# Entering the second block of a two-block network without a pause: modulation, the second stream's features and the final norm moved beside other work

## The reference

```python
def first_block(x, ...):
    for l in range(2):
        x = x + 0.5 * swiglu(rmsnorm(x, norm_ffn1[l]), w_ffn1_in[l], w_ffn1_out[l])
        ...                                      # mixer of three attentions
        x = x + 0.5 * swiglu(rmsnorm(x, norm_ffn2[l]), w_ffn2_in[l], w_ffn2_out[l])
    return rmsnorm(x, norm_final)

def second_block(x, c, ctx, c_ctx, ...):
    for i in range(2):
        sh1x, sc1x, g1x, sh2x, sc2x, g2x = silu(c) @ ada_w[i] + ada_b[i]      # 1024 x 6144
        sh1c, ... = silu(c_ctx) @ ada_w[i] + ada_b[i]
        hx = rmsnorm_2(x, norm_g[i, 0]) * (1 + sc1x) + sh1x
        hc = rmsnorm_2(ctx, norm_g[i, 0]) * (1 + sc1c) + sh1c
        if i == 0:      # Fourier mixing: fft2 over rows and groups of 256 columns, then fnet_wo
            x, ctx = x + g1x * fourier_mix(hx), ctx + g1c * fourier_mix(hc)
        else:           # RWKV, x alone is updated
            x = x + g1x * rwkv(hx, hc)
        x = x + g2x * ec_moe(rmsnorm_2(x, norm_g[i, 1]) * (1 + sc2x) + sh2x)  # 16 experts
        if i == 0:
            ctx = ctx + g2c * ec_moe(...)
    return rmsnorm_2(x, final_g)
```

## Time and profile before

| | us |
|---|---|
| median of 3 runs (lowest, highest) | 3563.28 (3561.82, 3569.27) |
| profiled execution, its own time | 3555.66 |
| its span, first to last instruction | 3553.6 |
| TensorE busy in it | 2912.4 (82%) |
| VectorE busy / ScalarE busy | 1184.2 / 973.2 |

### The profile page before, as it was taken

One profiled execution on the slowest core, in us unless ns is written; L12 is line 12 of the kernel. 1 busy time (PEld: TensorE's weight loads), 2 busy tenths in 40 slices (PEclk: granted clock), 3 DMA queues, 4 the chain that ended last, 5 costly groups with the idle time before them and its releaser, 6 DMA issues.

```text
span 3553.6 us, 63013 instructions
## 1 busy us (share of the span) xinstructions
PE 2912.4 (82%) x27818; PEld 1931.8 (54%) x27818; DVE 1184.2 (33%) x1569; ACT 973.2 (27%) x1474; POOL 179.9 (5%) x227
## 2 busy tenths in 40 slices
PE   8998999999989996798888873977878785677765
PEld 6776777787767774543333222436767673433322
DVE  4455565454555543130000014124343334100001
ACT  4445444343454441221000001013333330100000
POOL 0002000000020000000000000012221210000000
PEclk9999999999999998899999996989899898777787
DMA  6442345656423457029999981210000001699997
GB/s 246 169 178 98 114 172 190 238 194 248 153 104 128 178 195 288 8 71 399 421 421 421 421 337 80 95 64 9 8 9 14 8 4 40 269 421 421 421 421 300
DMA packets 100699, 708.62 MB, mean 199 GB/s; under 512 B 11572, under 2 KB 12340, under 8 KB 16992
## 3 DMA queue, kind: packets, MB, share of 16 engines
q1 hardware_dynamic: 94320, 682.34, 48.7%
q10 hardware_dynamic: 5472, 19.91, 1.6%
q0 software_dynamic: 656, 2.52, 0.2%
HBM read 703.65 MB, written 1.07 MB: 198 GB/s over the span
## 4 chain that ended last, share of the span: by engine, by line
PE 57%; DMA 21%; DVE 9%; issue 7%; ACT 4%; POOL 2%; SPq 0%; ACTq 0%; DVEq 0%; POOLq 0%
DMA weight_ring<-in_stream 19%; PE banks L536 7%; PE banks L538 7%; PE banks L537 7%; PE banks L1743 7%; PE banks L347 4%; PE banks L844 2%; PE banks L1619 2%; PE banks L846 2%; PE banks L845 2%; PE banks L2181 1%; PE banks L1651 1%; PE banks L2230 1%; PE banks L973 1%; ACT scratch L2547 1%
## 5 line engine op out<-in xcount | busy, mean ns | idle before, releaser
L1743 PE MATMUL banks<-weight_ring,scratch 128*32 128x256 f32 (+1 forms) x4608 | 630.5, 527 | 194.2 <-DMA weight_ring<-in_stream 190.4
L1743 PEld LDWEIGHTS banks<-weight_ring,scratch 128*32 128x32 f32 (+1 forms) x4608 | 200.8, 133 | 604.7 <-DMA weight_ring<-in_stream 301.6
L533 DVE TENSOR_TENSOR split_high<-weight_ring,split_high 128x1024 fp32r<-128x1024 f32 x198 | 243.4, 1230 | 272.3 <-ACT split_high L528 270.9
L528 ACT CAST split_high<-weight_ring 128x1024 fp32r<-128x1024 f32 x198 | 207.9, 1052 | 302.9 <-PE banks L538 265.8
L2547 ACT COPY scratch<-banks 128x1024 f32<-128x1024 f32 (+2 forms) x208 | 154.5, 766 | 306.1 <-PE banks L2234 126.7
L1167 DVE TENSOR_TENSOR split_high<-weight_ring,split_high 128x1024 fp32r<-128x1024 f32 x128 | 160.0, 1256 | 198.4 <-ACT split_high L1062 198.0
L1860 DVE TENSOR_TENSOR scratch<-scratch,banks 128x512 f32<-128x512 f32 (+1 forms) x32 | 17.7, 554 | 607.4 <-PE banks L1743 607.4
L536 PE MATMUL banks<-split_high,features_low 128*128 128x512 f32 x528 | 211.1, 400 | 3.3 <-DVE features_low L455 3.3
L538 PE MATMUL banks<-split_high,features_high 128*128 128x512 f32 x528 | 207.4, 393 | 0.0
L537 PE MATMUL banks<-split_high,features_high 128*128 128x512 f32 x528 | 207.2, 392 | 0.0
L844 PE MATMUL banks<-split_high,features_low 128*128 128x512 f32 x416 | 170.1, 409 | 19.5 <-DVE split_high L1167 16.2
(11 more groups left out here) (347 smaller groups left out, 4800.7 us busy)
## 6 DMA issues: line engine op xcount, KB each, us to landing
weight_ring<-in_stream SPq DMA_DIRECT2D x648, 1024.0 KB, 11.4
scratch<-in_pair_rows ACTq DMA_DIRECT2D x8, 448.0 KB, 3.8
scratch<-in_lora ACTq DMA_DIRECT2D x2, 1536.0 KB, 12.7
front<-in_gain_rows ACTq DMA_DIRECT2D x5, 512.0 KB, 4.2
bias<-bias_rows POOLq DMA_DIRECT2D x1, 2304.0 KB, 14.1
scratch<-in_routing ACTq DMA_DIRECT2D x2, 1040.5 KB, 5.1
scratch<-in_ada_b ACTq DMA_DIRECT2D x2, 768.0 KB, 3.9
resid<-in_x SPq DMA_DIRECT2D x2, 512.0 KB, 3.7
```

The lines of the kernel that those rows point to most:

```text
L528: act.copy(split[i % 4][0], source(i)).then_inc(*self.rounded.up())
L533: dve.tensor_tensor(lo, source(i), hi.bitcast(F32), ALU.subtract).then_inc(*self.rest.up())
L1743: last = pe.matmul(self.psum[q * M:(q + 1) * M, (GATE, UP, DOWN)[part], 0:W], left, w[:, j * D + q * W:j * D + (q + 1) * W], start=(k == 0 ...
```

## The change

- The modulation groups move: group 0 is now multiplied in stage 0, group 1 in stage 2, group 2 in stage 3, none in stage 5. Groups 3, 4 and 5 (24 chunks) all stand in front of RWKV: group 3 in `modulation_first`, groups 4 and 5 in `modulation_rest`, which is called between RWKV's norm and its features.
- A new class `Early` runs inside stage 5: it loads `ctx`, the bias, `norm_g`, the final gain and `dft`, finishes the modulation of layer 0, and makes the features `hT` of `ctx`. Its steps hang on the eleven groups of the up product by their number `n`.
- `fourier` has no `meet` in front any more. It transforms the eight pieces of `ctx` first, and does the last stage's `finish`, the final norm, the block's norm and the features of `x` beside them, row tile by row tile.
- The small tables `turns` of the mixer move to the tile `small`, and the saved modulation rows to `ada`.

```diff
+class Early:
+    def on_act(self, act, n):
+        if n == 0:
+            # six loads: ctx (2), ada_b, norm_g, norm_final, dft
...
+        elif n == 2:
+            act.wait_ge(p.consts_loaded.sem, self.consts)
+            for t in range(TT):
+                act.activation(self.xn[:, t, :], p.resid[:, (2 + t) * D:(3 + t) * D], ACT.Square, accum_out=self.sums[:, t:t + 1])\
+                    .then_inc(*self.up("ctx_squared"))
+        elif n == 3:
+            self.wait(act, "ctx_meant", 1)
+            act.activation(self.roots, self.sums, ACT.Sqrt).then_inc(*self.up("ctx_rooted"))
+        elif n in (6, 7):
+            t = n - 6
+            self.wait(act, "mod_ready", 1)
+            self.wait(act, "ctx_turned", t + 1)
+            for k in range(KT):
+                last = act.activation(self.hT[:, k, t * P:(t + 1) * P], p.psum[:, 6 + k // 4, (k % 4) * P:(k % 4 + 1) * P],
+                                      ACT.Identity, bias=p.modcol[:, 0, 1, k:k + 1], scale=p.scol[:, 0, 1, k:k + 1])
+            last.then_inc(*self.up("ctx_featured"))
+    def on_pe(self, pe, n):
+        if n in (3, 4):
+            if n == 3:
+                self.wait(pe, "mod_added", 1)
+            else:
+                self.wait(pe, "mod_copied", 2)
+            for g in ((0, 1), (2,))[n - 3]:
...
+                    last = pe.transpose(p.psum[:, 6 + g % 2, b * P:(b + 1) * P], self.mod[:, g, b * P:(b + 1) * P], p.ident[:, :])
+        elif n in (6, 7):
...
+                last = pe.transpose(p.psum[:, 6 + k // 4, (k % 4) * P:(k % 4 + 1) * P], self.xn[:, t, k * P:(k + 1) * P], p.ident[:, :])
+    def on_dve(self, dve, n):
+        if n == 2:
...
+            dve.tensor_tensor(self.mod_all, self.mod_all, self.bias, ALU.add).then_inc(*self.up("mod_added"))
+        elif n == 3:
+            self.wait(dve, "ctx_squared", 2)
+            dve.tensor_scalar(self.sums, self.sums, 1.0 / D, EPS, ALU.mult, ALU.add).then_inc(*self.up("ctx_meant"))
+        elif n in (4, 5):
+            for g in ((0, 1), (2,))[n - 4]:
+                self.wait(dve, "mod_turned", g + 1)
+                p.copy_mod(dve, g, 6 + g % 2).then_inc(*self.up("mod_copied"))
...
@@ ffn, TensorE / ScalarE (VectorE likewise, at the end of its group n)
             for n in range(1, groups):
+                if inner is not None:
+                    inner.on_pe(pe, n - 1)
                 if n >= 2:
                     pe.wait_ge(self.hid_done.sem, hid0 + n - 1)
...
                     self.save_bias(act, n - 2)
+                if inner is not None:
+                    inner.on_act(act, n)
@@ modulation
+    def modulation_groups(self, groups, chunk, bias, cT):
+            for i, g in enumerate(groups):
+                for k in range(KT):
+                    self.ada_chunk(pe, chunk + KT * i + k, k, cT, g)
+            for i, g in enumerate(groups):
+                pe.wait_ge(ve.sem, added0 + i + 1)
...
@@ fourier, TensorE
+            for i, (t, g) in enumerate(first):            # first: ctx's pieces, then x's
+                if i in (2, 5):
+                    turn(i // 3)
+                if i in (8, 12):
+                    wait(pe, self.parts_high, (i - 4) // 4)
+                if i >= 4:
+                    wait(pe, self.saved, i - 3)
@@ experts
-            if layer == 0:
-                for k in range(KT):
-                    self.ada_chunk(pe, a0 + k, k, self.silu_c, 0)
@@ rwkv_inputs
         self.norm_rows(range(n_t), xn)
+        self.modulation_rest()
         self.to_features(xn, hT, n_t, ...)
@@ run
-            self.ffn(3 * layer, ada=1 if layer else None)
+            self.ffn(3 * layer, ada=2 if layer else 0)
...
-            self.ffn(3 * layer + 2, ada=2 * layer)
+            self.ffn(3 * layer + 2, ada=None if layer else 1, inner=Early(self) if layer else None)
...
-        self.final_norm("norm_final", lambda t: self.resid[:, t * D:(t + 1) * D])
-        self.ada_group(3, before)
...
-        self.move_ada()
-        self.load_ctx()
-        self.modulation(0)
         self.experts(0, *self.fourier())
-        self.modulation(1)
+        self.modulation_first()
```

## The result

The changed kernel takes 3507.2 us (median of 4 runs, 3501.3 to 3513.89), the kernel before 3562.55 on the same chip (median of 4): a ratio of 0.9844, 95% interval 0.9827 to 0.9862. It is 55 us faster; forecast were 47, and 3516 in a range of 3503 to 3531. The profiled execution is 3501.3, its span 3499.3, against 3553.6. Left out of what follows are two of the four executions of experiment 4, 4225.53 and 3742.27 us, which ran at a mean granted clock of 0.675 and 0.79 where the other two had 0.91.

A forecast was written before the change was run, and what follows sets the result against it. TensorE was taken as busy for 82% of the span, so its standstills count, chiefly the break between the blocks. -71.6 + 0.8 + 9.8 - 5.7 + 19.8 = -46.9, from the median 3563.28 to 3516 us, range 3503 to 3531.

The forecast's parts named there:

- The break: Between stage 5's last matmul and the second transform: loads and waits leave the chain, 104.9 + 0.6 becomes 33.9, -71.6 us.
- the bound that the text had at 10.65: At the break: if TensorE finds its first piece only when the second tile is normed, the gain is 10.65 less, 61.
- The rival in which the seam waits for `x`: First transform: ScalarE's list holds up each piece, 10.65 more, up to 15: 3527 to 3531 us; chance 0.15.
- Stage 5: Group 2's chunks leave (-9.8); transposes (+3.1), a wait behind group 4 (+4.5) and slower clock (+3.0) come: +0.8 us.
- both terms: Behind group 4 of stage 5: a TensorE wait of 4.5 us, then 3.0 us for the lower clock.
- The rival of four waits: Stage 5: `Early` waits at each of its four places, three more of 7.5 each: 3538 us; chance 0.10.
- Stage 0: Group 0's eight chunks enter there in the same pattern, 8 x 1.23: +9.8 us.
- In front of RWKV: RWKV's entry: 16 more chunks must land before the features, so L290 starts at 2180.3 instead of 2160.55: +19.8 us.
- One sign: Between the last expert and RWKV's features the stream was to run at 421 GB/s without a pause.
- The experts' start: Layer 0's experts: group 3's eight chunks leave; first chunk used 14.2 later, 19.9 less to load: -5.7 us.
- lower bound of -9: At the experts' start: -9 us if the gather, which stands behind short waits, runs at a higher clock.

The follow-up runs named there:

- experiment 4: The kernel before, with only modulation group 3 moved from in front of layer 0's experts to in front of RWKV: 3567.88 and 3575.78 us.
- Experiment 3: The changed kernel with the first transform's pieces of `x` ahead of those of `ctx`: 3514.22 us, ratio 0.9873.
- experiment 1: The changed kernel with group 4 still multiplied ahead of RWKV's features and group 5 behind them: 3496.41 us, ratio 0.9805.
- experiment 6: The changed kernel with RWKV's four parameter loads issued earlier, ahead of the engines' meeting: 3507.92 us, ratio 0.9855.
- early loads: The changed kernel with RWKV's parameter loads issued ahead of the meeting; its three profiles took 794.6, 790.1 and 788.5 us from low-rank product to final projection.
- experiment 7: Four more profiles, two each of the changed kernel and that with earlier parameter loads: executions 3504.28, 3515.67, 3503.25 and 3501.41 us.

## Why the prediction was right

- **The break, -71.6: measured -72.4.** The list of waits came out as worked out: second tile normed at 10.0 (forecast 10.65), gates over at 33.4 (33.9). The features of `x`'s first tile, which hold up the second square, ended 7.6 behind the end of the stage (8.0). Experiment 3 shows that the order `ctx` first is worth 7 to 8 of it, the bound that the text had at 10.65. The rival in which the seam waits for `x` did not come.
- **Stage 5, +0.8: measured +0.4.** The wait was 4.5, as forecast, the clock behind it 0.52 for 5 us, and taking the wait away gave 7.2 against the 7.5 that both terms had. `Early`'s other three places did not wait: the list of TensorE's waits from 1180 to the end of the stage names L142 once, and L152 not at all. The Trainium skill ("ScalarE: Activation LUTs", What ACT_TABLE_LOAD costs) counts a drain of some 1.38 on top of a load of some 1.28, by which the wait would have been 5.9, an estimate; here the load of 1.28 starts 0.02 behind the cast, the silu 0.01 behind the load, and the wait is 4.5, so the measurement decides against the drain for this switch. Inside the 4.5 two sizes were off and cancelled: the load put the product 0.75 later and not 0.65, and the eight copies took 0.59 and not 0.8. (The rival of four waits had a slip in its sum: 3516.4 and three times 7.5 are 3539, not 3538.)
- **Stage 0, +9.8: measured +10.2.** That the two agree to 0.4 is in part luck: the end of stage 0 lies between 227.2 and 230.3 in seven profiles of kernels with the same code there.
- **In front of RWKV, +19.8: measured +20.7**, and +20.4 with group 3 alone moved (experiment 4). The bytes set it: experiment 1 takes eight of the 24 chunks out of the wait and wins 16, experiment 6 only fills idle transfer time and wins 6. One sign did not come: the stream was to run at 421 GB/s without a pause, and it ran at shares of 0.54 and 0.83 for the first 24 us (experiment 6 shows the two stretches). The sum did not suffer, since it was counted from a chunk that had the same pause ahead of it before (a share of 0.54 from 2111.00 to 2115.80).
- **The experts' start, -5.7: measured -12.5, with -1.0 in the experts themselves.** This is the term that was mis-sized, and nearly all of the 7.4 us between the sum and the profile; its lower bound of -9 was passed too. Its step said "from there the stream ran without a pause until the last expert", so that time saved ahead of the first expert would partly be lost to the stream. The stretches of before, from the first freed slot to behind the first expert:

```profile
1595.00:1603.50 8.50, 6.40 (x58) 1.40 (x49) 0.00 (x0) 0.06 (x1) 0.00 (x0) 1.00 0.88 335
1603.50:1617.00 13.50, 10.61 (x72) 10.34 (x68) 2.53 (x10) 6.13 (x17) 0.00 (x0) 0.75 0.98 410
1617.00:1624.00 7.00, 7.00 (x34) 2.88 (x36) 0.00 (x0) 1.18 (x1) 0.00 (x0) 1.00 0.57 172
```

and of after, at the same place:

```profile
1540.00:1547.00 7.00, 7.00 (x34) 2.34 (x34) 0.00 (x0) 1.11 (x2) 0.00 (x0) 1.00 0.55 206
```

  8.5 us at 335 GB/s and 13.5 at 410 are 8.4 MB, eight chunks: by 1617.0, when the first expert starts, all slots that group 3 had freed were full again, and the stream stood still for a part of the next 7 us (a share of 0.57), as it does after (0.55). So the ring is full at the first expert in both kernels, and from there to the last expert it takes 472 in both, and 471.8 to 473.2 in all fourteen profiles of this case (the -1.0 lies inside that). What is saved ahead of the first expert is saved in full: the chunks' stretch from 1594.01 to 1603.53 is 9.5, and the gather, which then runs at full clock, 10.33 - 7.43 = 2.9 more: 12.4. The bound of -9 had the gather's higher clock right and added it to the wrong base.
- **Not forecast, and no part of the change:** -2.9 in the stages 2 to 3 and +3.2 behind the features. In seven profiles of kernels with the same code there (the changed one four times, early loads three times) stages 2 to 3 took 679.6 to 683.1, and in the four profiles of the changed kernel it was 1393.4 to 1405.7 from the features to the end, most of that scatter in the stretch of experiment 7. So the profile's -54.3 is one draw: the changed kernel's four spans are 3499.3, 3499.4, 3506.8 and 3513.6, and that of before, 3553.6, was a low one too.

So -46.9 became -54.3: -7.8 at the experts (-12.5 and -1.0 against -5.7), the other four terms together +0.1, scatter +0.3. That is 7.4 of the 9.2 between the forecast 3516.4 and the measured 3507.2; most of the rest is that the profiled execution lies 5.9 below its median now, where it lay 7.6 below before.

## What to carry to other kernels

Where weights come as a stream through a ring, ask of each stall whether the ring is full at its end. Where it was, here, whatever shortened the stall was won in full, and the chunks taken out of the stream there were paid for where the ring ran empty: eight chunks gave 13 in one place and took 20 in the other. Before chunks are moved to a place that waits for bytes, split them by what the next instruction needs: 16 of the 24 chunks here were waited for and not needed, and moving eight of them behind the features shortened the entry by 16 us. A short wait of TensorE can cost more than its length, when it runs at its lower level afterwards: 4.5 us cost 7.2 here. And look for each gain in the median too: a stretch that got shorter by 6.5 us left it where it was.

## What the runs showed of the hardware

- The same 64 matmuls of the gather took 10.33 behind chunks of modulation with waits for the stream between them, at a mean granted clock of 0.75 from 1603.50 to 1617.00, and 7.43 at a clock of 1.00 where those chunks and waits are gone.
- The last of four loads of parameters took 22.10 from issue to landing while the stream went on beside it with groups 4 and 5, and 15.67 when six chunks were left to land.
- Waits of 1.69 and 4.37 us in front of the first transform, with eight transposes between them, made its first eight rows take 5.77 instead of 3.43.
- A table load for a switch from square root to silu took 1.28, with 0.02 ahead of it and 0.01 behind it.
- With identical instructions a stretch of 785 us varied by 10 from profile to profile, TensorE's busy time in it from 599.5 to 608.5 and its mean clock from 0.89 to 0.87. An edit that shortened the entry by 6.5 us is seen in that stretch, and not in the kernel's median.
